# A hybrid decoder step on one core: load stage rebuilt by token tile, state rows transposed inside the first mixer

## The reference

```
def rms_norm(x, g):
    y = xf * lax.rsqrt(jnp.mean(xf * xf, axis=-1, keepdims=True) + EPS) * g
...
def conformer_conv_module(x, prev, w_glu, b_glu, w_dw, b_dw, ln_g, ln_b, w_out, b_out):
    a, g = jnp.split(x @ w_glu + b_glu, 2, axis=-1)
    u = a * jax.nn.sigmoid(g)
    u_ext = jnp.concatenate([prev.astype(u.dtype), u], axis=1)
    c = depthwise_causal_conv(u_ext, w_dw) + b_dw
    c = jax.nn.silu(layer_norm(c, ln_g, ln_b))
    return c @ w_out + b_out, u_ext[:, -(CONV_A_WIDTH - 1):]
...
        hn = rms_norm(h, p['norm_mix_pre'][layer])
...
            m, st = conformer_conv_module(
                hn, conv_prev[layer], p['conv_w_glu'][layer], p['conv_b_glu'][layer],
```

## Time and profile before

| | |
|---|---|
| median of 3 runs | 3379.78 us |
| lowest and highest run | 3374.53, 3380.39 us |
| the profiled execution | 3380.21 us |
| its span | 3378.5 us |
| busy: TensorE, VectorE, ScalarE, GpSimd | 3210.0, 2003.3, 1384.1, 182.3 us |
| mean granted TensorE clock | 0.977 |

### The profile page before, as it was taken

The page is one execution under the profiler, slowest core; times in us unless marked ns, Lnnn a source line. Parts: engine busy times, 40 slices in busy tenths (PEclk is TensorE's granted clock), DMA queues, the critical chain, the costliest instruction groups (busy, mean ns, idle before and its releaser), DMA issues.

```text
span 3378.5 us, 64786 instructions
## 1 busy us (share of the span) xinstructions
PE 3210.0 (95%) x26182; PEld 2815.5 (83%) x26182; DVE 2003.3 (59%) x2967; ACT 1384.1 (41%) x2300; POOL 182.3 (5%) x345
## 2 busy tenths in 40 slices
PE   4998799999999999899799999999999999999998
PEld 3886699999999999899455555555589999999997
DVE  5899655653565445533666677676647554465533
ACT  3332434333333333323566666666534333333322
POOL 0000000000000002230100000000000000000000
PEclk8999899999999999999899999999999999999998
DMA  3111022333333335546699999999942333333332
GB/s 93 41 35 36 20 77 81 90 93 105 109 107 88 97 108 171 173 132 201 231 345 329 342 342 347 344 342 332 319 137 76 89 94 96 109 110 94 91 105 85
DMA packets 474188, 525.06 MB, mean 155 GB/s; under 512 B 18099, under 2 KB 395564, under 8 KB 473562
## 3 DMA queue, kind: packets, MB, share of 16 engines
q1 hardware_dynamic: 461684, 477.77, 43.2%
q0 software_dynamic: 12208, 43.16, 3.8%
HBM read 486.90 MB, written 33.95 MB: 154 GB/s over the span
## 4 chain that ended last, share of the span: by engine, by line
PE 46%; DVE 3%; ACT 2%; issue 1%; POOLq 0%; DVEq 0%; POOL 0%; DMA 0%; ACTq 0%
PE PS L815 25%; PE PS L1649 7%; PE PS L1662 4%; PE PS L1686 3%; PE PS L1716 2%; PE PS L1737 2%; PE PS L1726 2%; PE PS L1670 1%; DVE rems L1937 1%; ACT wt L1833 1%; ACT rest L1815 1%; DVE wq L1979 0%; DVE ws L1943 0%; DVE moA L894 0%; DVE hT L898 0%
## 5 line engine op out<-in xcount | busy, mean ns | idle before, releaser
L322 DVE TENSOR_TENSOR wlo<-raw,whi 128x1024 fp32r<-128x1024 f32 x368 | 450.6, 1225 | 614.8 <-ACT whi L318 601.7
L318 ACT CAST whi<-raw 128x1024 fp32r<-128x1024 f32 x368 | 386.0, 1049 | 944.8 <-PE PS L815 913.4
L815 PE MATMUL PS<-xfh,whi 128*128 128x264 f32 (+1 forms) x3072 | 634.0, 288 | 7.1 <-DVE xfl L911 6.8
L815 PE MATMUL PS<-xfl,whi 128*128 128x264 f32 (+1 forms) x3072 | 627.6, 286 | 0.0
L815 PE MATMUL PS<-xfh,wlo 128*128 128x264 f32 (+1 forms) x3072 | 626.8, 286 | 0.0
L815 PEld LDWEIGHTS PS<-xfh,whi 128*128 128x128 f32 x3072 | 480.8, 189 | 12.1 <-DVE xfl L911 7.6
L815 PEld LDWEIGHTS PS<-xfl,whi 128*128 128x128 f32 x3072 | 480.6, 189 | 0.0
L815 PEld LDWEIGHTS PS<-xfh,wlo 128*128 128x128 f32 x3072 | 480.4, 189 | 0.0
L815 PE MATMUL PS<-pA,whi 128*128 128x264 f32 x2048 | 333.0, 285 | 0.0
L1649 PEld LDWEIGHTS PS<-ident,kr 128*128 128x128 f32 x2048 | 220.8, 141 | 132.2 <-issue 130.0
L1926 DVE COPY kt<-PS 128x512 f32<-128x512 f32 x256 | 175.5, 686 | 244.3 <-PE PS L1649 243.9
(11 more groups left out here) (301 smaller groups left out, 5034.0 us busy)
## 6 DMA issues: line engine op xcount, KB each, us to landing
kr<-in_cache_k SPq DMA_DIRECT2D x256, 512.0 KB, 5.4
vr<-in_cache_v SPq DMA_DIRECT2D x256, 512.0 KB, 5.0
raw<-in_ffn_w_gate SPq DMA_DIRECT2D x88, 512.0 KB, 3.8
raw<-in_ffn_w_up SPq DMA_DIRECT2D x88, 512.0 KB, 3.8
raw<-in_ffn_w_down SPq DMA_DIRECT2D x64, 512.0 KB, 4.1
raw<-in_ffn_w_down SPq DMA_DIRECT2D x32, 384.0 KB, 3.4
raw<-in_conv_w_glu SPq DMA_DIRECT2D x16, 512.0 KB, 4.0
raw<-in_conv_w_out SPq DMA_DIRECT2D x16, 512.0 KB, 4.1
```

What stands on the lines that cost most here:

```text
L318: nc.scalar.copy(whi[b][:], raw[b][:]).then_inc(w_hi, 1)
L322: nc.vector.tensor_tensor(wlo[b][:], raw[b][:], whi[b][:].bitcast(F32), ALU.subtract).then_inc(w_lo, 1)
L815: mm = nc.tensor.matmul(PS[:, s + c, 0:c1 - c0], wt[t % RING][:, k, :], x(k0 + k)[:, c0:c1], start=start and k == 0 and wt is whi and x is hi,
```

## The change

Seven things change, all in the load stage and the first mixer.

- The prompt is loaded in eight transfers of one token tile each, with a semaphore each. TensorE transposes tile by tile (eight transposes for each), and VectorE alone copies each tile out.
- ScalarE squares the token tiles as they lie in xtok, with the sum of each row as a second output (ssum), and takes the root of 128x9. VectorE inverts 128x9 (L434 of the changed file), puts it on diagonals (L436, L439), TensorE multiplies by mean1 into PSUM banks 3 to 6 (L399), and the scaling reads the scale from there (L450). The factor 1024 of mean1 is taken out by scaling the root's argument, in the layer norm too, and the matrix of ones goes.
- The squares by block, their sums, the mean product, the 1056-wide root and reciprocal go.
- The first two weight tiles are issued ahead of the state rows, and their low parts stand ahead of the scaling on VectorE.
- The state rows are transposed in two groups of eight around the value product of block 0, and copied by ScalarE. The state windows of blocks 0 and 1 are copied after that.
- The FFN rows are transposed between the gate product of block 1 and the taps of block 0, and copied by ScalarE.
- The barrier after the load stage goes; srow and frow get places that are not overwritten before they are read.

```diff
     vrow = at("vrow", [NV, D], F32, AR_AT + (TT + 1) * 4096)
-    srow = at("srow", [120, 2, D], F32, AR_AT + (TT + 2) * 4096)
+    srow = at("srow", [120, 2, D], F32, AR_AT + 18 * ROW)
...
     xl32 = at("xl32", [P, KB, T], F32, AR_AT + 8 * ROW)
-    frow0 = at("frow0", [19, FF], F32, AR_AT + (TT + 2) * 4096 + 8192)
+    frow0 = at("frow0", [19, FF], F32, AR_AT + 20 * ROW)
...
         def load_sp(sp):
-            sp.dma_start(xtok[:, 0:TT, :], A["x_prompt"][0].rearrange("(t p) d -> p t d", p=P)).then_inc(ld_x, 16)
-            sp.dma_start(xtok[0:NS, TT, :], A["x_sample"].rearrange("b q d -> (b q) d")).then_inc(ld_x, 16)
+            for t in range(TT):
+                sp.dma_start(xtok[:, t, :], A["x_prompt"][0][t * P:(t + 1) * P, :]).then_inc(ld_x[t], 16)
+            sp.dma_start(xtok[0:NS, TT, :], A["x_sample"].rearrange("b q d -> (b q) d")).then_inc(ld_x[TT], 16)
             for r, src, n in vec_rows:
                 sp.dma_start(vrow[r:r + n, :], src).then_inc(ld_v, 16)
+            load_tile(sp, 0, 0, cols(w_glu, KB), KB)
+            load_tile(sp, 1, 1, cols(w_glu, 0), KB)
             st = A["state_conv_a"][0].rearrange("b s d -> (b s) d")
             for j in range(2):
-                sp.dma_start(srow[:, j, :], st[120 * j:120 * j + 120, :]).then_inc(ld_v, 16)
-            sp.dma_start(sbias[:, :], A["sb_bias"].broadcast_to([P, HEADS])).then_inc(ld_v, 16)
+                sp.dma_start(srow[:, j, :], st[120 * j:120 * j + 120, :]).then_inc(ld_s, 16)
+            sp.dma_start(sbias[:, :], A["sb_bias"].broadcast_to([P, HEADS])).then_inc(ld_s, 16)
             ffn_rows_dma(sp, 0, frow0)
             sp.dma_start(ptab[:, :], A["page_table"].rearrange("b n -> (b n)").rearrange("(a n) -> a n", a=1)).then_inc(s_tab, 16)
 
-        LD_V = 16 * (len(vec_rows) + 3)
+        LD_V = 16 * len(vec_rows)
+        w_glu = A["conv_w_glu"][0]
...
         def load_pe(pe):
             pe.wait_ge(cst, 2)
-            pe.wait_ge(ld_x, 32)
-            for k in range(KB):
-                if k >= 2:
-                    pe.wait_ge(tr_a, k - 1)
-                    pe.wait_ge(tr_v, k - 1)
-                for t in range(TT + 1):
-                    n = P if t < TT else NS
-                    mm = nc.tensor.transpose(PS[:, 3 * (k % 2) + t // 4, (t % 4) * P:(t % 4) * P + n],
+            for t in range(TT + 1):
+                n = P if t < TT else NS
+                pe.wait_ge(ld_x[t], 16)
+                if t >= 4:
+                    pe.wait_ge(tr_v, t - 3)
+                for k in range(KB):
+                    mm = nc.tensor.transpose(PS[:, 2 * (t % 4) + k // 4, (k % 4) * P:(k % 4) * P + n],
                                              xtok[0:n, t, k * P:(k + 1) * P], ident[0:n, 0:n])
                 mm.then_inc(tr_pe, 1)
             pe.wait_ge(ld_v, LD_V)
-            pe.wait_ge(tr_a, KB)
-            pe.wait_ge(tr_v, KB)
+            pe.wait_ge(tr_v, 6)
             for k in range(KB):
-                mm = nc.tensor.transpose(PS[:, 0, k * NV:(k + 1) * NV], vrow[:, k * P:(k + 1) * P], ident[0:NV, 0:NV])
+                mm = nc.tensor.transpose(PS[:, 2, k * NV:(k + 1) * NV], vrow[:, k * P:(k + 1) * P], ident[0:NV, 0:NV])
             mm.then_inc(tr_pe, 1)
+            pe.wait_ge(x_dg, 1)
+            pe.wait_ge(tr_v, TT)
+            for c in range(4):
+                mm = nc.tensor.matmul(PS[:, 3 + c, 0:CW2], mean1[:], spread[:, CW2 * c:CW2 * c + CW2], start=True, stop=True)
+            mm.then_inc(x_sp, 1)
+
+        def load_act(act):
+            act.wait_ge(cst, 2)
+            table("sqrt_and_others")
+            for t in range(TT + 1):
+                n = P if t < TT else NS
+                act.wait_ge(ld_x[t], 16)
+                if t >= 2:
+                    act.wait_ge(x_sq, t - 1)
+                nc.scalar.activation(junk[t % 2][0:n, :], xtok[0:n, t, :], ACT.Square, accum_out=ssum[0:n, t:t + 1]).then_inc(x_sq, 1)
+            act.wait_ge(x_sq, TT + 1)
+            nc.scalar.activation(std[:, 0:TT + 1], ssum[:], ACT.Sqrt, bias=eps_k[:, 0:1], scale=2.0 ** -30).then_inc(x_rt, 1)
+            table("sigmoid_and_others")
+            for b in range(2):
+                split_hi(act, b, 0, b)
             for k in range(KB):
-                for j in range(2):
-                    mm = nc.tensor.transpose(PS[:, 2 + k // 2, (k % 2) * 240 + j * 120:(k % 2) * 240 + j * 120 + 120],
-                                             srow[:, j, k * P:(k + 1) * P], ident[0:120, 0:120])
-            mm.then_inc(tr_pe, 1)
-            ffn_rows_pe(pe, 0, frow0)
-
-        def load_act(act):
-            for k in range(KB):
-                act.wait_ge(tr_pe, k + 1)
-                nc.scalar.copy(hT[:, k, 0:512], PS[:, 3 * (k % 2), :]).then_inc(tr_a, 1)
+                act.wait_ge(n_t, k + 1)
+                nc.scalar.copy(xh[:, k, :], xl32[:, k, :]).then_inc(n_hi, 1)
 
         def load_dve(dve):
-            for k in range(KB):
-                dve.wait_ge(tr_pe, k + 1)
-                nc.vector.tensor_copy(hT[:, k, 512:1024], PS[:, 3 * (k % 2) + 1, :])
-                nc.vector.tensor_copy(hT[:, k, 1024:T], PS[:, 3 * (k % 2) + 2, 0:NS]).then_inc(tr_v, 1)
-            dve.wait_ge(tr_pe, KB + 1)
-            nc.vector.tensor_copy(vec[:, :, :], PS[:, 0, 0:KB * NV].rearrange("p (k v) -> p k v", k=KB)).then_inc(g_wz, 1)
+            dve.wait_ge(cst, 2)
+            for t in range(TT + 1):
+                n = P if t < TT else NS
+                dve.wait_ge(tr_pe, t + 1)
+                j = 2 * (t % 4)
+                nc.vector.tensor_copy(hT[:, :, t * P:t * P + n],
+                                      PS[:, j:j + 2, :].rearrange("p c (a n) -> p (c a) n", a=4)[:, :, 0:n]).then_inc(tr_v, 1)
+            dve.wait_ge(tr_pe, TT + 2)
+            nc.vector.tensor_copy(vec[:, :, :], PS[:, 2, 0:KB * NV].rearrange("p (k v) -> p k v", k=KB)).then_inc(g_wz, 1)
             dve.wait_ge(g_wz, 1)
             nc.vector.tensor_tensor(wz[:, :, 0:EV - 1], vec[:, :, V_DW:V_DW + 2 * EV - 2:2], vec[:, :, V_DW + 1:V_DW + 2 * EV - 2:2], ALU.add)
-            nc.vector.tensor_copy(wz[:, :, EV - 1], vec[:, :, V_DW + CW - 1])
-            dve.wait_ge(tr_pe, KB + 2)
-            for k2 in range(KB // 2):
-                nc.vector.tensor_copy(stA[:, 2 * k2:2 * k2 + 2, :],
-                                      PS[:, 2 + k2, 0:480].rearrange("p (k v) -> p k v", k=2))
-            ffn_rows_dve(dve, 0)
...
+            nc.vector.tensor_copy(wz[:, :, EV - 1], vec[:, :, V_DW + CW - 1]).then_inc(g_wz, 1)
+            dve.wait_ge(x_rt, 1)
+            nc.vector.reciprocal(std[:, 0:TT + 1], std[:, 0:TT + 1]).then_inc(x_rs, 1)
+            dve.wait_ge(x_rs, 1)
+            nc.vector.tensor_tensor(spread[:, 0:NP].rearrange("p (t n) -> p t n", t=TT),
+                                    bass.AP(ident, 0, [(P, P), (0, TT), (1, P)]),
+                                    bass.AP(std, 0, [(TT + 1, P), (1, TT), (0, P)]), ALU.mult)
+            nc.vector.tensor_scalar(spread[:, NP:T], ident[:, 0:NS], std[:, TT:TT + 1], None, ALU.mult).then_inc(x_dg, 1)
+            for b in range(2):
+                split_lo(dve, b, b)
+            dve.wait_ge(x_sp, 1)
+            four = lambda ap: ap.rearrange("p (c w) -> p c w", c=4)
+
+            def low(k):
+                dve.wait_ge(n_hi, k + 1)
+                nc.vector.tensor_tensor(xl[:, k, :], xl32[:, k, :], xh[:, k, :].bitcast(F32), ALU.subtract).then_inc(n_lo, 1)
 
             for k in range(KB):
...
-        def apply_dve(dve, a, q, src, row, hi, lo, n, r0=0):
-            dve.wait_ge(n_rs, q + 1)
-
-            def low(k):
-                dve.wait_ge(n_hi, 8 * a + k + 1)
-                nc.vector.tensor_tensor(lo(k), tmp[k % 2][:, 0:n], hi(k).bitcast(F32), ALU.subtract).then_inc(n_lo, 1)
-
-            for k in range(KB):
-                if k >= 2:
-                    dve.wait_ge(n_lo, 8 * a + k - 1)
-                nc.vector.scalar_tensor_tensor(out=tmp[k % 2][:, 0:n], in0=src(k), scalar=vec[:, k, row:row + 1],
-                                               in1=rs[:, r0:r0 + n], op0=ALU.mult, op1=ALU.mult).then_inc(n_t, 1)
+                nc.vector.scalar_tensor_tensor(out=four(xl32[:, k, :]), in0=four(hT[:, k, :]), scalar=vec[:, k, V_MIX_PRE:V_MIX_PRE + 1],
+                                               in1=PS[:, 3:7, 0:CW2], op0=ALU.mult, op1=ALU.mult).then_inc(n_t, 1)
                 if k >= 1:
                     low(k - 1)
             low(KB - 1)
...
-            for m in range(KB):
+            for m in range(1, KB):
...
+                else:
+                    pe.wait_ge(f_ft, 1)
...
+            def state_rows(r):
+
+                pe.wait_ge(ld_s, 48)
+                if r == 1:
+                    pe.wait_ge(st_a, 1)
+                for k in range(4 * r, 4 * r + 4):
+                    for j in range(2):
+                        c0 = (k % 2) * 240 + j * 120
```

(42 more changed lines are left out.)

64 lines of the change are left out of this document (14 added, 50 removed).

## The result

| | before | changed |
|---|---|---|
| median of the runs | 3378.98 us (4 runs, 3374.53 to 3380.39) | 3353.28 us (4 runs, 3349.19 to 3355.14) |
| profiled execution, time and span | 3380.2, 3378.5 us | 3355.14, 3353.2 us |
| ratio | | 0.9921, 95% interval 0.9909 to 0.9932 |

The changed kernel is 25.7 us faster by the medians, 0.8%. The forecast was 3352 us, 1.3 us from the median; it had a gain of 27.9 us.

A forecast was written before the change was run, and what follows sets the result against it. A serial prologue precedes a VectorE-bound first mixer. The first product moving from 63.84 to 32.9 us gains 30.9, less 0.9 and 2.1 put back: 27.9 off 3380.2 gives 3352 us, range 3345 to 3359.

The forecast's parts named there:

- V = 22.0: Load stage: time the vector rows land, 22 us, including 1 us added for a slower shared queue; bounds 17 to 28.4.
- rival 2: Load stage: vectors land early, about 17 us, the slow engine carrying mostly state and FFN rows; total 3347.3 us; chance 0.13.
- the lonely engine: Load stage: one DMA engine of 16 working alone some 6.1 us, its excess of about 140 KB taken as the vectors'.
- The transposes, copies and squares are cover: Load stage: prompt work ends by 20.3 us at the latest, squares and root by 17, hidden behind the vector rows' landing.
- From V to the scaling 7.04 us: Load stage: from vector rows landing to scaling, 1.65 us for transposes and paired taps plus 5.39 for the scale's steps.
- S = 32.9: End of load stage: start of the first product in the changed kernel, 32.9 us, where it was 63.84 before.
- Second weight tile at 25.1, hidden by 1.6 us: Load stage: second weight tile lands at 25.1 us; cast and low part hide if it lands by 26.7.
- Rival 1: Load stage: weight tiles land no earlier than before, 30.9 us, and delay the first product to 37.1; total 3356.5; chance 0.15.
- 0.9 put back ahead of the value product: Block 0: eight state transposes between gate and value products make the gate multiplication 0.93 us later.
- 2.1 in block 0: Block 0: remaining state transposes and FFN rows ahead of the tap sums make VectorE wait 2.1 us, paid once.
- The multiplication at 65.7, the layer norm 28 us earlier: Expected signs in the changed profile: block 0's gate multiplication at 65.7 us, layer norm about 28 us earlier.
- Rival 3: Load stage: prompt transfers pay one after another, not overlapping; first product at 66.5 us, total 3385.9, slower; chance 0.02.

The follow-up runs named there:

- Experiment 3: The changed kernel with the 31 tap rows loaded as 30 rows and 1 row; 3349.27 us.
- experiment 2: The changed kernel with the first two weight tiles issued behind the state and FFN rows, as before the change; 3356.27 us.
- experiment 7: The changed kernel with the scale's reciprocal, spread and four products written ahead of the vectors' transposes and copies on VectorE and TensorE; 3351.85 us.
- experiment 8: The changed kernel with 34 unread transposes of a constant on TensorE while it waits for the vectors; 3353.05 us.
- experiment 1: The changed kernel with the prompt loaded again as one transfer of 4 MB; 3358.86 us.
- experiment 9: The changed kernel with SyncE waiting for each prompt tile to land before issuing the next; 3370.74 us.
- experiment 6: The changed kernel with sums of squares spread first, then root and reciprocal over 1056 columns, and scaling read from SBUF; 3364.06 us.
- experiment 4: The changed kernel with the second group of state rows moved to block 1 and the FFN rows to block 3, ahead of the gate product; 3357.3 us.

## Why the prediction was right

By its own steps:

- *What bounds.* A serial prologue ahead of a stretch that VectorE fills: right. Of the 30.55 us at the multiplication of block 0, block 0 takes back 2.49 (35.33 us where it took 32.84) and everything from there to the layer norm 0.25, 0.22 of it in the wait for the means.
- *V = 22.0*: 22.20 measured, and the reason held. Experiment 3 removes the excess and finds the vectors at 17.97, near rival 2's 17, but not for rival 2's reason: the lonely engine carried the tap rows. The last microsecond of V was a guess and its closeness is partly luck: the vectors come at 24.60 us when state rows follow them in the queue instead of weights (experiment 2), and at 21.64 in experiment 7, which edits no load.
- *The transposes, copies and squares are cover*: right, over at 17.5 us, against 20.3 at the latest.
- *From V to the scaling 7.04 us*: 7.57. The vectors' transposes took 1.09 us instead of 0.67 and the scale's products 3.89 with TensorE's granted clock at 0.50, which I had not priced; in experiment 8 the two take 0.69 and 3.08.
- *Scaling to first product 3.86 us*: 3.86, and reading the second operand from PSUM cost nothing. A block of scaling even got shorter, 2.40 us where it took 2.53, which gave 0.8 us over the eight blocks.
- *S = 32.9*: 33.63.
- *Second weight tile at 25.1, hidden by 1.6 us*: the weakest step. Its sum started from 21 us where V had been put at 22; with 22 the margin is 0.6. The tile was cast only at 26.93; its low part ended 0.54 us before the scaling began. The tile did not follow the vectors at 1.5 us each but took 2.9 behind the first, where it was issued ahead of the state rows; in experiment 2, where the state rows are issued ahead of both tiles, 1.5 separate the two casts. That the state rows take the difference is likely and was not tried alone. Rival 1 was nearer than its 0.15 said; experiments 7 and 8 both end at it.
- *0.9 put back ahead of the value product*: the eight transposes added 0.74 us. *2.1 in block 0*: 2.05 measured, with a wait of 0.25 for the weights beside it that I had not foreseen. Nothing in block 1: right.
- *The multiplication at 65.7, the layer norm 28 us earlier*: 65.12 and 27.8 us. Two misses cancel here: the first product came 0.7 us later than S, and from there to the multiplication it took 31.49 us where 31.8 and 0.9 had been counted (the shorter scaling gives 0.8 of the 1.2, the cheaper transposes 0.2, the rest was not traced).
- *27.9 us in total*: 27.8 at the layer norm, 25.3 in the profiled execution's span. Most of the rest, 2.2, is the clock of another stretch, in seven of the eleven profiles of the changed kernel and its edits and in neither of the two of the kernel before; it is within the range but not in the sum. Against the medians the gain is 25.7, so the sum was 2.2 too high, and the time came within 1.3 us partly because it was reckoned from the profiled execution, 1.2 us above the median of before.
- *Rival 3.* The Trainium skill, DMA: Bandwidth & Descriptors, section Rules for kernel authors, asks for at least 1 MiB per DMA for full bandwidth, and so for one transfer of 4 MB over eight of 512 KB. Experiments 1 and 9 show when that holds here: with their landings overlapping, the eight bring the first product 2.7 us earlier than the one; waited for one at a time, they bring it 19 us later. The estimate of 3.2 us for such a piece alone (2.0 us plus 512 KB over 436 GB/s) stands beside 3.5 us measured; the same page of the Trainium skill fits that formula, in its section Anatomy of one DMA — SWDGE (gpsimd) path, to transfers that GpSimd issues, and these are issued by SyncE.
- *The lonely engine.* The Trainium skill, DMA: Bandwidth & Descriptors, section Why a DMA increments its semaphore by 16 and not by 1 ties the number of engines to the slowest dimension of more than one element, so one engine for 31 rows and 15 for 30; experiment 3, with 30 rows and 1 in place of 31, agrees in 4.2 us of landing time. Of a single row the rule is less plain than the prediction has it, and no run here tries one.

Of the 30.2 us at the first product, 2.7 are the waits per tile (experiment 1), 8.2 the narrow root and reciprocal (experiment 6) and 3.8 the weights' place in the queue (experiment 2); these were each measured against the rest of the change and need not add. The remaining 15 or so belong to what no experiment undid: the row sums on tokens, which replaced squares and additions of 128x1056, the state and FFN rows moved out of the prologue, and the dropped barrier. These were not taken apart.

## What to carry to other kernels

Follow the arrival of the smallest loads as closely as that of the largest: a transfer of 31 rows of 4 KB held up vectors and the weights behind them for over 4 us, but only once the work that had covered it was gone. Root and reciprocal belong before a broadcast, where they have nine columns and not 1056. When work is moved into an engine's slack, measure the slack of everything queued behind it on each engine that it touches (here the cast of the next weight tile, not the tap sums), and put it where the engine does not have to wait for its turn: in experiment 4 TensorE's clock was lower behind each such wait, and the moves cost 10.1 us of waits for the 2.05 that they removed.

## What was not expected of the hardware

- TensorE's granted clock fell to 0.50 within the 6.3 us in which it waited for vectors, and was 1.00 again only after 38 us, with unbroken work from 33.6 us on; it fell as well in experiment 3, where the wait was 2.12 us (0.62 in 18 to 22 us, 0.50 in 22 to 25); filling the gap with 34 transposes kept it at 1.00 to 25 us and cut the eight 128x264 matmuls from 3.89 to 3.08 us.
- The prompt's transposes took 1.94 to 1.97 us for eight when each tile was waited for, and 1.09 us for eight in experiment 3 (from 12.26 us), while the granted clock read 1.00 in both. The vectors' transposes of experiment 9 took 1.09 us at a reading of 1.00 too, as in the changed kernel at 0.50: in these runs the reading did not tell the two paces apart until its first fall.
- Scaling and low part take 2.40 us a block where they took 2.53. The PSUM operand is not the reason: experiment 6 reads SBUF and has 2.40 as well. What is left is that the scaled block now has a place of its own for each k, where two alternating tiles waited for the low part of two blocks back; that was not tried by itself.
